# Gate rows by one transpose and a trip through DRAM; sums closed by their last product; one weight block loaded in halves

## The reference

```python
mod = jax.nn.silu(c) @ w + b
shift, scale, gate = jnp.split(mod, 3, axis=-1)
...
h = (h + gate * m).astype(x.dtype)      # m: S5 mixer (layer 0), forgetting attention "fox" (layer 1)
...
f = conv_ffn(hn, ffn_w_up[i], ffn_conv_w[i], ffn_conv_b[i], ffn_w_down[i])
h = (h + gate * f).astype(x.dtype)
```

## Time and profile before

| | us |
|---|---|
| median of 3 runs | 1318.82 |
| lowest, highest | 1313.47, 1320.58 |
| the profiled execution's own time | 1316.12 |
| its span, first to last instruction | 1314.3 |
| PE busy | 1191.1 (91%) |
| DVE busy | 669.4 (51%) |
| ACT busy | 462.2 (35%) |
| POOL busy | 168.1 (13%) |
| mean granted TensorE clock | 0.954 of full speed |

### The profile page before, as it was taken

The page is one execution under the profiler, slowest core; times in us unless marked ns, Lnnn a source line. Parts: engine busy times, 40 slices in busy tenths (PEclk is TensorE's granted clock), DMA queues, the critical chain, the costliest instruction groups (busy, mean ns, idle before and its releaser), DMA issues.

```text
span 1314.3 us, 22196 instructions
## 1 busy us (share of the span) xinstructions
PE 1191.1 (91%) x8874; PEld 851.7 (65%) x8874; DVE 669.4 (51%) x1207; ACT 462.2 (35%) x746; POOL 168.1 (13%) x270
## 2 busy tenths in 40 slices
PE   8999899887789877787999999999999989999996
PEld 5646554432335323332877889999969767999995
DVE  3677452231211221121486757676675766667675
ACT  5463421010100001002654454444455545443343
POOL 0000115572343032101020000000000000000000
PEclk9999899898987899798999999999999999999998
DMA  9865599999999999999786465555456241554441
GB/s 372 356 222 244 230 404 418 430 428 428 428 428 428 428 429 428 429 428 428 291 349 231 161 272 203 181 191 191 176 193 240 82 160 49 187 192 184 178 178 40
DMA packets 38389, 371.81 MB, mean 283 GB/s; under 512 B 4133, under 2 KB 7742, under 8 KB 14398
## 3 DMA queue, kind: packets, MB, share of 16 engines
q1 hardware_dynamic: 34462, 365.47, 68.8%
q10 hardware_dynamic: 3872, 5.57, 1.2%
HBM read 369.94 MB, written 1.08 MB: 282 GB/s over the span
## 4 chain that ended last, share of the span: by engine, by line
PE 66%; DMA 23%; DVE 5%; ACT 3%; issue 2%; POOL 1%; DVEq 0%; SPq 0%; ACTq 0%
PE ps L705 64%; DMA ring<-in_w_up 20%; DMA ring<-in_ada_w 2%; PE ps L936 1%; DMA ring<-in_fox_out 1%; DMA ring<-in_s_out 1%; ACT XH L1617 1%; DVE X L2774 1%; DVE ring_parts L516 1%; ACT XH L1575 0%; PE ps L712 0%; DVE W L2955 0%; DMA X<-in_x 0%; PE ps L948 0%; DVE XH L2773 0%
## 5 line engine op out<-in xcount | busy, mean ns | idle before, releaser
L705 PE MATMUL ps<-W_parts 128*128 128x256 f32 (+2 forms) x2672 | 383.9, 305 | 3.9 <-DVE W_parts L2898 2.0
L705 PEld LDWEIGHTS ps<-W_parts 128*128 128x128 f32 x2672 | 356.8, 191 | 28.0 <-issue 4.1
L705 PE MATMUL ps<-ring,W 128*32 128x512 f32 (+2 forms) x1512 | 239.3, 679 | 55.2 <-DMA ring<-in_w_up 29.1
L705 PEld LDWEIGHTS ps<-ring,W 128*32 128x32 f32 (+1 forms) x1512 | 62.1, 124 | 190.8 <-issue 114.6
L705 PE MATMUL ps<-W 128*32 128x64 f32 (+7 forms) x1696 | 135.6, 290 | 23.9 <-DVE W L2755 12.8
L705 PEld LDWEIGHTS ps<-W 128*32 128x32 f32 (+5 forms) x1696 | 85.6, 152 | 78.3 <-issue 70.8
L2743 DVE COPY W<-ps 128x1024 f32<-128x1024 f32 x16 | 19.6, 1224 | 191.4 <-PE ps L705 191.4
L2856 DVE TENSOR_TENSOR W_parts<-ring,W_parts 128x2048 fp32r<-128x2048 f32 x44 | 100.8, 2292 | 26.2 <-ACT W_parts L1942 26.0
L705 PEld LDWEIGHTS ps<-kc,W 128*128 128x128 f32 x648 | 85.7, 212 | 28.2 <-DVE W L2743 17.4
L705 PE MATMUL ps<-kc,W 128*128 128x32 f32 (+2 forms) x648 | 88.1, 293 | 10.2 <-DVE W L2743 9.4
L705 PE MATMUL ps<-XH_parts,ring_parts 128*128 128x256 f32 x512 | 94.0, 286 | 2.1 <-ACT XH_parts L1578 1.9
(11 more groups left out here) (395 smaller groups left out, 1353.5 us busy)
## 6 DMA issues: line engine op xcount, KB each, us to landing
ring<-in_w_up SPq DMA_DIRECT2D x32, 2048.0 KB, 25.7
ring<-in_w_down SPq DMA_DIRECT2D x32, 2048.0 KB, 23.7
ring<-in_w_gate SPq DMA_DIRECT2D x29, 2048.0 KB, 24.0
ring<-in_ada_w SPq DMA_DIRECT2D x24, 2048.0 KB, 10.1
ring<-in_up SPq DMA_DIRECT2D x44, 1024.0 KB, 5.8
ring<-in_dn SPq DMA_DIRECT2D x44, 512.0 KB, 3.3
ring<-in_fox_in SPq DMA_DIRECT2D x6, 2048.0 KB, 7.9
ring<-in_w_o SPq DMA_DIRECT2D x2, 2048.0 KB, 15.7
```

The source lines that it names most:

```text
L705: return pe.matmul(o, l, r, start=a, stop=z_, skip_group_check=True, **kw)
```

## The change

Three things are changed.

1. Gate rows. `gate_rows`, its four calls and ScalarE's three copies are gone. In their place `gate_turn(a, b, ready, bank)` on TensorE turns the columns 24a+16 to 24b of `mod` with one transpose (8, 32 or 8 columns); `gate_written` on ScalarE copies the turned rows out of PSUM and writes them to `gate_dram`, one row of 128 numbers (512 bytes) for each; `gate_spread` reads the 8 rows of one gate as 1024 numbers into all 128 partitions, by ScalarE's queue. Turned are layer 0 (after the second session's turn in the S5 stage), layers 1 and 2 together (between glu(1,0) and glu(1,1)) and layer 3 (after fox_out(1,0)). VectorE waits for the spreads where it waited for the copies, and once more before the sums of the fox stage. On ScalarE gate_written(3, 4) stands after fox_high(7) and before the load of the final gains and ffn(1). Around the S5 gate rows the order of the halves changes too: glu(0,1), glu(1,0), glu(1,1).
2. Closed sums. The last product of each output sum carries the stop flag itself, and the four products of zeros are gone.
3. Block ("s5", 5) is loaded by two transfers of half the columns, and ScalarE splits its first half once that has landed. The semaphore `w_in_half` is named `half_filled` and used for both.

```diff
@@ -247,6 +247,7 @@
     sums_dram = nc.dram_tensor("forget_sums", [FH, T], F32).ap()
+    gate_dram = nc.dram_tensor("gate_rows", [LAYERS * 24, P], F32).ap()
@@ -502,8 +503,11 @@
             name = APART[n]
-            act.wait_ge(filled_sem[slot_of[name]], filled_at(*name))
             for half in halves:
+                if name == ("s5", 5) and half == 0:
+                    act.wait_ge(S("half_filled"), 32)
+                else:
+                    act.wait_ge(filled_sem[slot_of[name]], filled_at(*name))
                 a = slice(half * SLOT // 2, (half + 1) * SLOT // 2)
@@ -622,7 +626,7 @@
                         h = NC // 2 * n
-                        sp.dma_start(ring[:, s, 0:h], w_in[:, 0:h]).then_inc(S("w_in_half"), 16)
+                        sp.dma_start(ring[:, s, 0:h], w_in[:, 0:h]).then_inc(S("half_filled"), 16)
                         sp.dma_start(ring[:, s, h:2 * h], w_in[:, h:2 * h]).then_inc(filled_sem[s], 16)
@@ -673,7 +677,13 @@
                 elif name == "s5":
-                    load(begin(name, i), SLOT, block((s5_in, s5_glu, s5_out)[i // 2], i % 2))
+                    src = block((s5_in, s5_glu, s5_out)[i // 2], i % 2)
+                    if i == 5:
+                        s = begin(name, i)
+                        sp.dma_start(ring[:, s, 0:SLOT // 2], src[:, 0:SLOT // 2]).then_inc(S("half_filled"), 16)
+                        sp.dma_start(ring[:, s, SLOT // 2:], src[:, SLOT // 2:]).then_inc(filled_sem[s], 16)
+                    else:
+                        load(begin(name, i), SLOT, src)
                 elif name == "up0":
@@ -788,12 +798,12 @@
-            def gate_rows(layer, banks):
-
-                for c in range(NC):
-                    last = mm(ps[:, banks[c // 4], (c % 4) * P:(c % 4) * P + P],
-                              mod[:, layer, 16 + c:17 + c].to_broadcast([P, P]), ident, True, True)
-                last.then_inc(S("gate_mm"), 1)
+            def gate_turn(a, b, ready, bank):
+
+                pe.wait_ge(S("mod_ready"), ready)
+                m0, m1 = 24 * a + 16, 24 * b
+                pe.transpose(ps[0:m1 - m0, bank, 0:P], mod[:, :, :].rearrange("p l m -> p (l m)")[:, m0:m1], ident
+                             ).then_inc(S("line_mm"), 1)
@@ -1329,6 +1339,7 @@
             ada_turn(2)
+            gate_turn(0, 1, 1, 6)
             bu(1)
@@ -1347,16 +1358,14 @@
-            glu(1, 0)
-            pe.wait_ge(S("mod_ready"), 1)
-            pe.wait_ge(S("ada_kept"), 5)
-            gate_rows(0, (6, 7))
             pe.wait_ge(S("y_low"), 2)
             glu(0, 1)
+            glu(1, 0)
+            gate_turn(1, 3, 2, 6)
             glu(1, 1)
-            pe.wait_ge(S("gate_copied"), 1)
+            pe.wait_ge(S("ada_kept"), 5)
             for t in range(NT):
@@ -1418,22 +1427,16 @@
                         n, t = (i4 % 2, i4 // 2) if closing else (i4 // 2, i4 % 2)
-                        for g, w in ((gh, dh), (gl, dh), (gh, dl)):
+                        for j, (g, w) in enumerate(((gh, dh), (gl, dh), (gh, dl))):
                             last = mm(ps[:, 4 + 2 * n + t, :], g[:, b, t * P:t * P + P],
-                                      w[:, b, BANK * n:BANK * n + BANK], False, False)
-                        if closing and i4 < 3:
-                            closed(4 + 2 * n + t)
-                    last.then_inc(S("down_mm"), 1)
-                    if closing:
-                        closed(7)
-
-                def closed(b):
-
-                    mm(ps[:, b, :], zb[0:1, 0:P], zb[0:1, :], False, True).then_inc(S("ffn_mm"), 1)
+                                      w[:, b, BANK * n:BANK * n + BANK], False, closing and j == 2)
+                        if closing:
+                            last.then_inc(S("ffn_mm"), 1)
+                    if not closing:
+                        last.then_inc(S("down_mm"), 1)
                 up(0, 0, True)
-                gate_rows(2 * k + 1, (2, 3))
                 with pe.Fori(0, NF // 2 - 1) as i:
@@ -1498,12 +1501,10 @@
             values(0, 0, 0, 0, NC)
-            gate_rows(2, (2, 3))
             values(1, 0, 1, 0, NC)
             pe.wait_ge(S("nf_ready"), FH // 2)
-            pe.wait_ge(S("gate_copied"), 3)
@@ -1522,6 +1523,7 @@
             fox_out(1, 0, 2)
+            gate_turn(3, 4, 3, 1)
             fox_out(1, 1, 3, 0, 4)
@@ -1592,6 +1594,20 @@
+
+            def gate_written(a, b, bank, n):
+
+                m0, m1 = 24 * a + 16, 24 * b
+                rows_ = K("ones")[0:m1 - m0, :]
+                act.wait_ge(S("line_mm"), 4 + n)
+                own(act.activation(rows_, ps[0:m1 - m0, bank, 0:P], ACT.Copy))
+                act.dma_start(gate_dram[m0:m1, :], rows_).then_inc(S("gate_written"), 16)
+
+            def gate_spread(dst, layer, written):
+
+                act.wait_ge(S("gate_written"), 16 * written)
+                act.dma_start(dst, bass.AP(gate_dram.tensor, (24 * layer + 16) * P, [[0, P], [1, D]])
+                              ).then_inc(S("gate_copied"), 16)
@@ -1900,6 +1916,7 @@
             ada_keep(2)
+            gate_written(0, 1, 6, 1)
@@ -1921,15 +1938,14 @@
             act.activation(XNr[:, 4:8, :], HT[:, 4:8, :], ACT.Copy).then_inc(S("y_high"), 1)
+            gate_spread(GBs, 0, 1)
             apart_high(act, 4)
-            act.wait_ge(S("gate_mm"), 1)
-
-            act.activation(GBs.rearrange("p (b n) -> p b n", b=2), ps[:, 6:8, :], ACT.Copy
-                           ).then_inc(S("gate_copied"), 1)
             for j in range(4):
                                ACT.Sigmoid).then_inc(S("glu_sig"), 1)
+                if j == 1:
+                    gate_written(1, 3, 6, 2)
             apart_high(act, 5)
@@ -1945,7 +1961,7 @@
                     if not first:
-                        act.wait_ge(S("down_mm"), i * 2 + (NF * k + b - 1))
+                        act.wait_ge(S("down_mm"), i * 2 + ((NF - 1) * k + b - 1))
                     act.activation(dh[:, b, :], ffn_raw("down", k, b), ACT.Copy
@@ -1964,9 +1980,7 @@
                 down_high(0, 0, True)
-                act.wait_ge(S("gate_mm"), layer + 1)
-                act.activation(GB.rearrange("p (b n) -> p b n", b=2), ps[:, 2:4, :], ACT.Copy
-                               ).then_inc(S("gate_copied"), 1)
+                gate_spread(GB, layer, 2 + k)
@@ -1998,6 +2012,7 @@
             ada_keep(5)
+            gate_spread(GBx, 2, 2)
             for j in range(4):
@@ -2027,9 +2042,6 @@
             apart_high(act, 12)
-            act.wait_ge(S("gate_mm"), 3)
-            act.activation(GBx.rearrange("p (b n) -> p b n", b=2), ps[:, 2:4, :], ACT.Copy
-                           ).then_inc(S("gate_copied"), 1)
             values_copied(1)
@@ -2054,6 +2066,7 @@
+            gate_written(3, 4, 1, 3)
             act.wait_ge(S("scores_mm"), 16)
@@ -2847,7 +2860,7 @@
                 apart_low(v, 5, half)
-            v.wait_ge(S("gate_copied"), 1)
+            v.wait_ge(S("gate_copied"), 16)
@@ -2911,7 +2924,7 @@
                 tiles(NF // 2 - 1, False)
-                v.wait_ge(S("gate_copied"), layer + 1)
+                v.wait_ge(S("gate_copied"), 16 * (layer + 1))
                 for j in range(4):
@@ -2974,6 +2987,7 @@
             fox_low(7)
+            v.wait_ge(S("gate_copied"), 48)
```

More of the change, by code:

```diff
@@ L814, in _ @@
             wz = ring[:, slot_of["w_in", 0], :].rearrange("p (c n) -> p c n", c=NC)
-            pe.wait_ge(S("w_in_half"), 16)
+            pe.wait_ge(S("half_filled"), 16)
             pe.wait_ge(S("ht_act"), 1)
```

## The result

The changed kernel takes 1321.96 us (median of 9 executions, 1318.22 to 1326.96); the kernel before, beside it on the same chip, takes 1315.96 (9 executions, 1311.80 to 1320.58). The ratio is 1.0039, 95% interval 1.0020 to 1.0057: slower by 0.39%, or 5.1 us. The forecast was 1321.9 us and +3.1 us. The time was hit, in part by luck: the difference was forecast too small, by 2.0 us against the ratio and by 2.9 against the two medians (6.0 apart), and the base of 1318.82, which was 2.9 above the later median, made up for it.

What follows compares the result with a forecast made beforehand. TensorE was taken to bound the kernel, with two thirds of the chain of work. Terms -3.4 - 0.6 + 0.1 + 5.5 + 1.5 = +3.1 us, on the 1318.82 us median, gave 1321.9 us; range 1314.5 to 1328.

Steps and rivals of the forecast that it cites:

- Gate rows in the feed-forward blocks: Start of both feed-forward blocks: 1.70 us of gate products leave TensorE at each, -3.4 us together; the spreads' transfers stay hidden.
- Closing: End of each feed-forward block: VectorE's first gated sum comes 0.32 us sooner, twice -0.3 us.
- Third site: Before the attention's scores: TensorE waits for VectorE's mask sums, so removed products lengthen the wait to 2.6 us; 0 gain.
- S5: S5 stage: 2.6 us pause, -1.7 gate products, +0.2 transpose, 1.01 us stall gone; sum +0.1, bounds -0.9 to +1.2.
- The wait on ScalarE: Before the second feed-forward block: ScalarE's queue waits for a transpose, delaying turn(4,0) and products; +5.5 us, bounds +3.5 to +6.
- rival (1): Before the second feed-forward block: ScalarE's added wait isn't felt, the rest holds; -3.9 us, 1314.9 us; chance 0.12.
- The clock behind it: TensorE from turn(4,0): half-rate stretch of about 3 us after the pause; +1.5 us, bounds 0 to +3.9.
- The sum: Whole kernel: all terms together, +3.1 us against the profiled execution; chance of the forecast 0.60.
- (2): Whole kernel: all four gate sites, the closing and the stall give their full gain; -7.8 us, 1311.0 us; chance 0.05.
- (4): Whole kernel: the removed products were filler within waits, so only the added wait counts; +7.0 us, 1325.8 us; chance 0.06.
- (3): S5, attention's start and turn(4,0): pauses from 2.6 us each bring half-rate clock; +8.0 us, 1326.8 us; chance 0.17.

Runs made afterwards that it cites:

- e8: The kernel before with the closed sums alone, the last product closing each feed-forward sum; one execution at 1312.12 us.
- e9: e5 with 9 products of the identity that nobody reads before the attention's scores; 1310.59 us, ratio to the kernel before 0.9941.
- e2: The changed kernel with the S5 halves in their old order, glu(1,0) before glu(0,1); 1318.80 us, ratio to the kernel before 0.9994.
- e6: e5 with the last S5 output block loaded by one transfer instead of two halves; 1311.31 us, ratio to the kernel before 0.9957.
- e11: The kernel of e5 unchanged, measured a second time; 1312.67 us, ratio to the kernel before 0.9953.
- e3: The kernel before plus one ScalarE wait for the third fox_out group, ahead of the final gains' load and ffn(1); 1322.52 us, ratio 1.0048.
- e7: e5 with unread products of the identity, 8 before turn(3,0) and 9 before the attention's scores; 1307.96 us, ratio to the kernel before 0.9942.
- e10: e5 with 8 products of the identity that nobody reads before turn(3,0) alone; 1311.63 us, ratio to the kernel before 0.9952.
- e5: The changed kernel with gate_written(3,4) behind ffn(1)'s first squares and the S5 halves in their old order; 1312.68 us, ratio to the kernel before 0.9961.
- e4: The changed kernel with unread products of the identity, 8 before the S5 y_low wait and 20 before turn(4,0); 1317.11 us, ratio to the kernel before 0.9987.
- e1: The changed kernel with gate_written(3,4) moved on ScalarE behind the squares of ffn(1)'s first 128 rows; 1315.06 us, ratio to the kernel before 0.9980.

## Why the prediction was right, step by step

The outcome (within 0.5%) and the time came out as forecast, and the cause as well: the wait on ScalarE in front of the second feed-forward block eats what the two blocks gain. The difference was not so well forecast: the clock was priced too low in three places. The steps:

**Gate rows in the feed-forward blocks.** Forecast with the closing -2.0 in each; measured -2.08 and -2.07 (C and H). The spreads, one wide broadcast each, are issued from 772.2 on and, by the view of the tile `gate_rows`, every transfer of the gate rows lands within 9.4 us; C and H have no room for a gated sum that waits for one.

**Closing.** Forecast -0.3 each; -0.31 and -0.28 (e8).

**Third site.** Forecast that the pause before the scores grows to 2.6 at no gain. The row after is 2.56 where the earlier trace rows had 0.90:

```profile
1038.47 1.34 PE L715 MATMUL ps<-W 64*128 64x128 f32 x16 [2.56 <-DVE W L2968]
```

That VectorE is last there held. That the longer pause costs nothing held nearly: it lengthens the first slow stretch of the attention, by 0.1 to 0.7 us of work (e9). D as a whole grew by 0.47, and I had not looked at another place in it. The turn of the rows before the values, turn(3,0), now waits 2.13 us for ScalarE, where it waited 0.54 before. It is the products of zeros that are missing ahead of it: e8, which closes the sums and changes nothing else, has the same pause.

```profile
967.53 2.77 PE L722 MATMUL ps<-kc,W 128*128 128x128 f32 x12 [2.13 <-ACT W L1569]
...
964.29 0.98 PE L712 MATMUL ps<-kc,W 128*128 128x128 f32 x7 [2.15 <-ACT W L1562]
```

The first row is the changed kernel's, and the windows above show the clock at 0.58 there; the second is e8's.

Two things move D, and together they account for all thirteen values. The first is this clock: it fell to half rate at the turn in four of the nine executions with the pause of 2.1 us (the changed kernel, e2, e6, e11: D is 78.5 to 78.8), and in none of the four with 0.55 us or less (before, e3, e7, e10). The second isn't the granted clock, which is 1.00 in both cases: the dense products of the features come in groups of three, and a group starts every 0.360 us in before, e5, e9 and e10 (22 groups from 995.05 to 1002.97 before), where D is 78.0 to 78.1, and every 0.353 us in the others, but for parts of e4 and e11 (23 groups from 994.74 to 1002.87 in the changed kernel), where D without the slow turn is 77.2 to 77.3. The two spacings are worth 0.8 us of D. e3 and e8 have the old gate rows and 0.353, so the change has no part in that; its cause is open. So the +0.47 is a price of the change, about 1.35 us of clock at turn(3,0) in this execution, less 0.85 us that the execution before happened to lose. The forecast had no term for this place.

**S5.** Forecast +0.1, measured +1.10. The pause was forecast 2.6 and is 2.47; the stall went, as said; the gate products went; the transpose added 0.12 from start to start, not 0.2, as it is a single record. What failed was to price the clock here at nothing and to leave it to the third rival. e4, with the clock kept up, has B at 49.30, which is 0.40 below the kernel before; the changed kernel is 1.50 above e4. The forecast's term without the clock was right to 0.5 us, and the clock made the difference: 1.50 us in this execution, 2.68 in e1's. The block's transfer was forecast some 5 us sooner and came 3.4 sooner, counted from VectorE's low part. The argument that the halves matter little, since the block arrives in time, held for the order of the change, in which it is issued early; e6 shows that with the old order they matter by 0.9.

**The wait on ScalarE.** Forecast +5.5 at turn(4,0), measured +5.58, and +4.83 from the bare wait of e3, which has neither copy nor issue behind it. That rival (1), the wait not felt, was wrong is shown by e1 as well: the wait is felt where it stands, and costs nothing where the copy comes 4.7 us later (1102.67, not 1097.96).

**The clock behind it.** Forecast +1.5 of 0 to 3.9, measured +2.33 (G; 2.29 by e4). It was mis-sized because I took the length of the slow stretch from the one pause in the earlier trace rows, about 3 us; here the window from 1104 to 1111 is at 0.51 and covers both the turn and the products behind it, nearly 5 us of work.

**The sum.** -2.08 - 2.07 + 1.10 + 5.58 + 2.33 = +4.9 where I had +3.1. D with +0.47 and E with -1.29 bring the ledger to the span's +4.3 with A's +0.26. E's gain isn't the change's: its products are the same, e5 and e11 differ by 2.9 us there, and the execution before has a second slow stretch in the attention, from 1071 us on the earlier trace rows, which the changed kernel's lacks.

**The rivals.** (2) needed both waits to vanish, and they didn't. (4), that the products removed were filler, fell by C and H. (3), the clock after every pause, was half right. Its condition holds, that a pause of about 2.6 us is enough for a drop: both executions with the open S5 pause, the changed kernel's and e1's, have a half-rate stretch behind it, and none of the other eleven has. Of its prices, 1.7 in S5 was fair (1.50 and 2.68), 2 more than I took at turn(4,0) was too high (0.8), and so was 1.2 before the scores (0.1 to 0.7); it too had nothing at turn(3,0).

The Trainium skill (TensorE: Matmul & The Clock Gate, section "HAM oscillation — how this bites in real kernels") describes a kernel that waits some 3 to 5 us for a DMA ahead of each tile's products, and says that each next tile then starts at the low clock. The pause of 5.31 us agrees: the eight records of turn(4,0) right behind it took 1.97 us where they took 1.03 before. The S5 pause is shorter than the waits of that page, and behind it both kinds of start are seen: e1's first pair is slow, while in the changed kernel the first 1.5 us run at the full rate, and the drop comes in the middle of the work.

## What to carry to other kernels

On an engine that works in order, a wait delays all that is queued behind it. Before a wait is added, list the instructions behind it and find the place in the queue where that engine stands idle anyway; here this was worth 7.8 us for one call. A step that frees the busiest engine is only a gain where that engine doesn't stand waiting right after: in the changed kernel two of the four sites gave 1.7 us each and the other two gave pauses. The S5 site gives its share too once the order is the old one (B is 2.96 below before in e2, with the stall of 1.01 gone as well); the site before the scores never does. And where a stage that the edits hardly touch varies by 12 us, a ledger of stages of the same two marks finds 0.3 us that whole times can't.

## What the runs showed of the hardware

Behind the S5 pause of 2.47 us the granted clock fell to half rate both times that it stood open. In the changed kernel it didn't fall at once: products ran at full rate for 1.5 us, then at half rate, with TensorE busy all the time. In e1 it was low already when the products resumed. Behind a pause of 2.1 us at turn(3,0) it fell in four of nine executions. The attention is a stage of many short waits, and there it fell within 2 us of the scores behind each pause of 2.56 us, and later, or in e7 not at all, behind one of 0.56 to 0.90. How long a pause has to be isn't settled by this.

Products that nobody reads, put into a pause, kept the clock at 1.00 (e4), and what followed was quicker by 1.5 us after one pause and 2.3 after the other. They cost nothing that the stages show where they end before the wait does, as here (F is 15.12 with and without them).

Where the slow stretches fall changes from one execution to the next of the same kernel. The attention of e5 and e11, the same code, took 52.38 and 55.30 us. In e5:

```profile
1036.00:1044.00 8.00, 6.64 (x37) 4.97 (x38) 6.06 (x34) 5.08 (x25) 0.00 (x0) 0.57 0.00 0
1066.00:1074.00 8.00, 5.37 (x43) 4.32 (x44) 7.90 (x24) 4.88 (x19) 0.00 (x0) 1.00 0.57 235
```

The second of its windows is at 1.00 where that of e11 is at 0.57. One profile of such a stage is one draw: e7's undisturbed attention looked like the fillers' work until e9 and e10.
